# A routed-expert block: the slot's weight moves into the up rows, and the scattering matmuls are split into two FP32R parts

## The reference, cut to what matters

```python
g_onehot = one_hot(argmax(g_logits)); p_group = sum(softmax(g_logits) * g_onehot)
top_v, top_i = top_k(softmax(e_sel), 2); top_v = top_v / sum(top_v)
comb = g_onehot * w_local * p_group          # 0 but for the token's two experts
for g in range(N_GROUPS):
    a = silu(h @ w_gate[g]) * (h @ w_up[g])  # per expert, D_EXPERT = 256 columns
    a = a * comb[:, :, g, :, None]
    out = out + a @ w_down[g]
x = x + gate2 * out
```

## Time and profile before

| | |
|---|---|
| median of 3 runs | 501.27 us (500.9 to 501.34) |
| profiled execution, first to last instruction | 499.3 us |
| what lies around the span, against the median | 1.97 us |
| TensorE busy | 481.4 us, 96% |
| the windows, first to last gate/up start | 294.99 to about 486.8 us |
| one window where nothing waits | 5.31 us |
| bytes moved | 162.02 MB, 324 GB/s over the span |

### The profile page before, as it was taken

How to read it: one execution, slowest core, us unless ns; L and a number is a source line. 1 busy time by engine, 2 the same in 40 slices (tenths; PEclk the granted TensorE clock), 3 DMA queues, 4 the chain that set the end, 5 groups by cost and what they waited for, 6 DMA issues and landing times.

```text
span 499.3 us, 14059 instructions
## 1 busy us (share of the span) xinstructions
PE 481.4 (96%) x5769; PEld 378.1 (76%) x5770; DVE 241.3 (48%) x647; ACT 136.6 (27%) x243; POOL 152.8 (31%) x195
## 2 busy tenths in 40 slices
PE   8899999999999999999999999999999999888895
PEld 6678888888888888888888877767767766556563
DVE  1433765656565656456651455344344344332343
ACT  4013122323222232313232362232232232221231
POOL 0000010101010101010100018777777777665673
PEclk9999999999999999999999999999999999998998
DMA  8999318295969590907073999899999999999992
GB/s 324 423 424 425 164 53 379 58 433 202 427 258 425 219 407 25 408 8 296 42 291 130 362 411 430 358 394 422 434 437 427 421 441 427 421 423 428 424 403 95
DMA packets 13711, 162.02 MB, mean 324 GB/s; under 512 B 1648, under 2 KB 1904, under 8 KB 3568
## 3 DMA queue, kind: packets, MB, share of 16 engines
q1 hardware_dynamic: 13392, 161.04, 78.1%
q10 hardware_dynamic: 288, 0.52, 0.3%
HBM read 160.51 MB, written 1.05 MB: 324 GB/s over the span
## 4 chain that ended last, share of the span: by engine, by line
PE 83%; DMA 14%; DVE 2%; ACT 0%; issue 0%; ACTq 0%; DVEq 0%
PE ps L536 79%; DMA wex<-in_ex 14%; PE ps L839 1%; PE ps L879 1%; PE ps L840 1%; DVE work L958 0%; ACT xT L528 0%; PE ps L755 0%; PE ps L753 0%; PE ps L754 0%; DVE act L973 0%; DVE act L961 0%; PE ps L739 0%; ACT work L431 0%; DVE work L1223 0%
## 5 line engine op out<-in xcount | busy, mean ns | idle before, releaser
L536 PE MATMUL ps<-act,wmix 128*128 128x256 f32 x864 | 195.0, 381 | 1.7 <-DVE act L973 1.7
L536 PEld LDWEIGHTS ps<-act,wmix 128*128 128x128 f32 x864 | 161.1, 190 | 25.9 <-issue 4.6
L412 POOL TENSOR_SCALAR work<-trig,work 128x256 f32<-128x256 f32 x70 | 64.9, 937 | 57.3 <-issue 48.1
L398 POOL TENSOR_TENSOR work<-work,trig 64x256 f32<-64x256 f32 x8 | 5.8, 719 | 237.0 <-ACT work L466 141.6
L536 PE MATMUL ps<-work 32*128 32x256 f32 (+6 forms) x864 | 72.8, 374 | 0.6 <-DVE work L1223 0.6
L536 PE MATMUL ps<-wex,work 128*32 128x128 f32 (+1 forms) x1824 | 65.6, 295 | 3.7 <-DMA wex<-in_ex 3.7
L536 PEld LDWEIGHTS ps<-wex,work 128*32 128x32 f32 x1824 | 49.8, 110 | 16.8 <-issue 8.4
L536 PEld LDWEIGHTS ps<-work 32*128 32x128 f32 (+3 forms) x864 | 47.6, 168 | 13.3 <-issue 3.3
L524 ACT ACTIVATE work<-ps 128x64 f32<-128x64 f32 x35 | 7.8, 224 | 139.9 <-PE ps L879 139.9
L524 ACT ACT_TABLE_LOAD x35 | 44.9, 1283 | 1.8 <-issue 0.3
L416 POOL TENSOR_TENSOR work<-work,trig 128x512 f32<-128x512 f32 x35 | 44.5, 1271 | 0.0
(11 more groups left out here) (200 smaller groups left out, 432.2 us busy)
## 6 DMA issues: line engine op xcount, KB each, us to landing
wex<-in_ex SPq DMA_DIRECT2D x10, 3072.0 KB, 22.4
wex<-in_ex SPq DMA_DIRECT2D x10, 2048.0 KB, 24.1
wex<-in_ada SPq DMA_DIRECT2D x8, 2048.0 KB, 7.7
wmix<-in_ex SPq DMA_DIRECT2D x4, 3072.0 KB, 20.9
wmix<-in_mix_odd SPq DMA_DIRECT2D x4, 3008.0 KB, 15.5
wmix<-in_mix_even SPq DMA_DIRECT2D x3, 3200.0 KB, 16.1
wex<-in_ex SPq DMA_DIRECT2D x9, 1024.0 KB, 11.4
wex<-in_ada SPq DMA_DIRECT2D x8, 1024.0 KB, 16.7
```

What stands on the lines that cost most here:

```text
L398: nc.gpsimd.tensor_tensor(k_sq[0:ROPE, :], k_sq[0:ROPE, :], k_rope_sq[0:ROPE, :], ALU.add).then_inc(sq_joined, 1)
L412: nc.gpsimd.tensor_scalar(comb_both[:, rows], slot_row[:, rows], lane_now, None, ALU.is_equal).then_inc(comb_half, 1)
L536: return nc.tensor.matmul(out, lhsT, rhs, start=start, stop=stop, **kw)
```

## The change

- **Weight.** `comb` is no longer multiplied with `weight_row`; line 416 goes, and `comb` holds zeros and ones. Instead a column per window, `row_scale`, holds 1 in the gate partitions (0 to 63) and the slot's weight in the up partitions; DVE's copy at line 1208 becomes a product with column n of it.
- **Making row_scale.** Ahead of its loop POOL turns the four slot numbers of each partition's tokens into window and lane (five short operations, each waiting for the one ahead), then into two one-hot sets, of 32 lanes (four operations) and of 48 windows times the weight (four operations). TensorE multiplies them (8 matmuls of M=32, N=48) in the place of `spread(2, ...)`, and ACT copies 64 x 48.
- **Scattering.** DVE writes the down result times gate rows to `y_full`, copies it to `y_high` in FP32R and subtracts to `y_low` in FP32R; `comb` is FP32R too. `combine` multiplies low and high part with `comb`: 16 source matmuls in place of 8.
- Around it: three zeroing copies and a memset in place of one memset ahead of the router, `bound` at least 1 in TensorE's registers, `slot_no` 48 wide, and 8 KB for the DMA scratch.

```diff
-        ycomb = piece(2 * T)
-        y_sb, comb = ycomb[:, 0:T], ycomb[:, T:2 * T]
+        row_scale = sb("row_scale", [P, WINDOWS])
+        y_high, y_low, comb = (sb(n, [P, T], F32R) for n in ("y_high", "y_low", "comb"))
+        slot_row, y_full = trig[:, 0:2 * T], trig[:, 2 * T:3 * T]
@@ POOL, ahead of its loop
+            pool.wait_ge(slot_tok_ready, 1)
+            nc.gpsimd.tensor_scalar(win_no, slot_of, 1.0 / WIN, 0.5 / WIN - 0.5, ALU.mult, ALU.add).then_inc(pool_step, 1)
+            pool.wait_ge(pool_step, 1)
...
+            for a in range(4):
+                nc.gpsimd.tensor_scalar(lane_oh[:, a, :], co("slot_no")[:, 0:WIN], lane_of[:, a:a + 1], None, ALU.is_equal).then_inc(scale_in, 1)
+            pool.wait_ge(w_tok_ready, 1)
+            for a in range(4):
+                nc.gpsimd.tensor_scalar(win_oh[:, a, :], co("slot_no"), win_no[:, a:a + 1], w_of[:, a:a + 1], ALU.is_equal, ALU.mult).then_inc(scale_in, 1)
@@ POOL, in its loop
-                nc.gpsimd.tensor_tensor(comb_both, comb_both, weight_row, ALU.mult).then_inc(comb_pair, 1)
@@ ACT
-            nc.scalar.copy(weight_row, ps[:, 2, :]).then_inc(spread_copied, 1)
+            nc.scalar.copy(row_scale[P // 2:, :], ps[P // 2:, 2, 0:WINDOWS]).then_inc(spread_copied, 1)
@@ TensorE
-                return mm(ps[:, 4 + q, h * T:(h + 1) * T], y_sb[q * WIN:(q + 1) * WIN, h * P:(h + 1) * P], comb[q * WIN:(q + 1) * WIN, :],
-                          False, True, skip_group_check=True)
+                for y in (y_low, y_high):
+                    last = mm(ps[:, 4 + q, h * T:(h + 1) * T], y[q * WIN:(q + 1) * WIN, h * P:(h + 1) * P], comb[q * WIN:(q + 1) * WIN, :],
+                              False, True, skip_group_check=True)
+                return last
-            pe.wait_ge(w_tok_ready, 1)
-            spread(2, s_work[:, 8:10, :])
+            pe.wait_ge(scale_in, 8)
@@ DVE, in its loop
-                v.tensor_copy(gu_sb, ps[:, 0, 0:P]).then_inc(gu_copied, 1)
+                v.tensor_scalar(gu_sb, ps[:, 0, 0:P], row_scale[:, bass.ds(n, 1)], None, ALU.mult).then_inc(gu_copied, 1)
-                v.tensor_tensor(y_sb, ps[:, 2, 0:T], gate_rows, ALU.mult).then_inc(y_copied, 1)
+                v.tensor_tensor(y_full, ps[:, 2, 0:T], gate_rows, ALU.mult).then_inc(y_step, 1)
+                v.tensor_copy(y_high[:], y_full).then_inc(y_step, 1)
+                v.tensor_tensor(y_low[:], y_full, y_high[:].bitcast(F32), ALU.subtract).then_inc(y_copied, 1)
```

More of the change, by code:

```diff
@@ L8 @@
 U32 = mybir.dt.uint32
+F32R = mybir.dt.float32r
 ACT = mybir.ActivationFunctionType
@@ L35 @@
                 ("b_router", 36), ("w_router", KT * 36), ("gate_rows", T))
-CONST_WIDTHS = (("ident", P), ("before", P), ("swap", P), ("slot_no", WIN), ("lane_no", 1), ("mask", T),
+CONST_WIDTHS = (("ident", P), ("before", P), ("swap", P), ("slot_no", EXPERTS + 2 * T // WIN), ("lane_no", 1), ("mask", T),
                 ("group_no", GROUPS), ("less_magic", EXPERTS), ("fold", 37), ("inv_freq", 1))
@@ L170, in block_kernel @@
         logits_t, sq_sums = hT[:, 4, :], hT[:, 5, :]
+        lane_oh = comb_both[:, 0:4 * WIN].rearrange("p (a n) -> p a n", a=4)
+        win_oh = comb_both[:, 4 * WIN:4 * WIN + 4 * WINDOWS].rearrange("p (a n) -> p a n", a=4)
+        win_no, lane_of = comb_both[:, 2 * T - 8:2 * T - 4], comb_both[:, 2 * T - 4:2 * T]
         rs_tok, r_tok = s_work[:, 10, :], s_work[:, 11, :]
@@ L405, in _ @@
             with pool.Fori(0, windows_before(pool, EXPERTS)) as n:
-                pool.wait_ge(comb_pair, n * 2 + 1)
+                pool.wait_ge(comb_pair, n + 1)
                 pool.wait_ge(comb_ready, n + 1)
@@ L415, in _ @@
                 nc.gpsimd.tensor_scalar(lane_now, lane_now, float(WIN), None, ALU.add).then_inc(comb_pair, 1)
-                nc.gpsimd.tensor_tensor(comb_both, comb_both, weight_row, ALU.mult).then_inc(comb_pair, 1)
-                pool.wait_ge(comb_pair, n * 2 + 3)
                 pool.wait_ge(combined, n + 1)
-                nc.gpsimd.tensor_tensor(comb, comb_both[:, 0:T], comb_both[:, T:2 * T], ALU.add).then_inc(comb_ready, 1)
+                nc.gpsimd.tensor_tensor(comb[:], comb_both[:, 0:T], comb_both[:, T:2 * T], ALU.add).then_inc(comb_ready, 1)
         @block.scalar
@@ L861, in next_bound @@
                 pe.reg_mov(bound_at, bound)
-                pe.reg_mov(bound, bound_next)
+                pe.reg_alu(bound, bound_next, 1, ALU.max)
             def window(place, use, n, following, at_tail=False):
@@ L895, in _ @@
             pe.reg_mov(bound_at, 0)
-            pe.reg_load(bound, table[0:1, 1:2])
+            pe.reg_load(bound_next, table[0:1, 1:2])
+            pe.reg_alu(bound, bound_next, 1, ALU.max)
             turn_rows(0)
-            pe.wait_ge(w_tok_ready, 1)
-            spread(2, s_work[:, 8:10, :])
+            pe.wait_ge(scale_in, 8)
+            for a in range(4):
+                for q in (2, 3):
+                    last = mm(ps[q * WIN:(q + 1) * WIN, 2, 0:WINDOWS], lane_oh[:, a, :], win_oh[:, a, :], a == 0, a == 3)
+            last.then_inc(spread_ready, 1)
             ROUNDS = EXPERTS // EX_SLOTS
@@ L1111, in _ @@
             merge(HEADS - 1)
-            v.memset(ycomb, 0.0).then_inc(y_copied, 1)
+            v.memset(row_scale[0:P // 2, :], 1.0)
+            link(v.memset(zeros[:], 0.0))
+            for y in (y_high, y_low, comb):
+                last = v.tensor_copy(y[:], zeros[:].broadcast_to([P, T]))
+            last.then_inc(y_copied, 1)
             v.memset(wins[:, 0:1], 0.0)
@@ L1249, in constants @@
     put("lane_no", (r % WIN).astype(np.float32)[:, None])
-    put("slot_no", np.broadcast_to(np.arange(WIN, dtype=np.float32), (P, WIN)))
+    put("slot_no", np.broadcast_to(np.arange(WINDOWS, dtype=np.float32), (P, WINDOWS)))
     mask = np.zeros((P, T), np.float32)
```

27 lines of the change are left out of this document (20 added, 7 removed).

## The result

| | before | after |
|---|---|---|
| median | 501.3 us (500.9 to 501.98, 4 runs) | 510.53 us (509.94 to 512.72, 4 runs) |
| ratio | 1 | 1.0187, 95% interval 1.0162 to 1.0212 |
| span of the profiled execution | 499.3 us | 508.1 us |
| first gate/up | 294.99 | 303.28 |
| first refill of weights issued | 297.01 | 306.61 |

The account below looks back on a forecast made before the run. DMA is full and the end hangs on the last weights' landing. Start +1.55 and five combines at -0.41 move the issue by -0.50, the last gate/up by -1.13; with +0.05 at the end 500.2 us, range 498.4 to 503.8.

Parts of the forecast that it names:

- The start of the windows: Ahead of the first window, TensorE waits for POOL instead of running spread(2): first gate/up 1.55 us later, bounds 0.8 and 3.
- POOL's chain: POOL's operations making row_scale ahead of the loop: 2.1 plus 2.64 us from slots ready, so TensorE starts at 296.0.
- The clock: Rival: TensorE's clock drops after a wait, ahead of the last gate/up or at 294 us; costs 1.7, 501.9 us; chance 0.22.
- What bounds the kernel: In the windows DMA is full; early TensorE savings close a DMA hole at 322 to 326 us and pull landings in.
- The scattering matmuls: Each window's combine in one-pass FP32R takes 0.66 us instead of 1.07, 0.41 saved.
- no gain per combine: Rival: FP32R takes two passes, or low and high part on one row tile block the next; 503.7 us; chance 0.14.
- DVE and POOL in the window: In each window, DVE's added operations fit under existing cover and POOL's dropped product was not waited for: nothing.
- The last part: Behind the last gate/up: two combines at -0.41 each and y's two further DVE operations at +0.87, sum +0.05 us.
- Waits for weights: Sign: TensorE waits for weights about ten times, over 20 us in all, instead of 7.
- the hole closes entirely: Rival: start late by 0.8, combines shorter by 0.6, DMA hole at 322 us gone; 498.3 us; chance 0.12.

Follow-up runs that it names:

- the shortened kernel: The changed kernel with five warming matmuls of 512 columns instead of ten of 256, 20 TensorE instructions fewer ahead of the loop: 503.2 us, ratio 1.003.
- the one without padding: The changed kernel without the head_slot padding that puts the head of TensorE's outer loop at the start of a block of 256 instructions: 503.39 us.
- the kernel before with the wait: The kernel before with POOL's 13 new operations ahead of its loop, TensorE's wait for them and one register step more: 503.44 us.
- the weight alone: The shortened kernel with combine in float32 and one y as before, row_scale and the product in the copy kept: 504.69 us, ratio of four runs 1.0056.
- one of eight combine matmuls: The kernel before with seven of the eight combine matmuls left out in each window, the last combine whole: 498.07 us.
- the split alone: The kernel before with y in low and high part and 16 FP32R combine matmuls; weight_row, spread(2) and POOL's product kept: 500.06 us, ratio 0.9964.
- the version that beats both: The shortened kernel with row_scale made by eight POOL and two DVE operations, the last combine taking high parts first: 500.57 us, ratio 0.9974.
- changed, shortened, 20 put back: The shortened kernel with 20 TensorE instructions put back at the start as five matmuls of one column: 510.76 us.

## Why the prediction was wrong, point by point

**The start of the windows** is the step that failed. It gave +1.55 us, bounds 0.8 and 3; measured are +8.29 for the first gate/up and +9.6 for the first refill. Three things were wrong in it.
- *The branch, 6.0 us.* The term priced the eight small matmuls by their duration (0.5 us, measured 0.53) and not by the room that they take. The order showed 16 records more ahead of a loop with `head_slot` in it, and neither the step nor a rival asked what the padding does when code grows. The branch's 0.32 us could have been read from the trace of before. No bound from rows would have held 6 us, but a rival "the loop's head moves by a block" belonged in the list.
- *POOL's chain, +0.7 us.* TensorE was to start at 296.0 and started at 296.68, of which 0.31 are the prologue. The operations of 4 columns took 0.20 to 0.33, as expected from 0.22, and the gaps between them 0.1 instead of 0.20. The plain form took 0.36 for 32 columns instead of 0.31, the two-operation form 0.53 for 48 columns instead of 0.35, inside the bound ("at double").
- *The clock, 1.3 us.* The rival had it "in the new 2 us wait at 294 us" at 1.34 for a gate/up. In the changed kernel it came with 6 us of idle time, 1.31. After 2.2 us of idle time it came in the profiled executions of the shortened kernel and of the one without padding, and didn't in that of the kernel before with the wait, nor in the weight alone; so its chance is open, its price is right.

**What bounds the kernel** was right: DMA full, last landing 37.7 us behind its issue, the end hanging on it by a lag of TensorE that vanished (0.12 us). The kernel with most of each combine left out shows it best. The other half of the step, that all landings follow the issue behind the sixth gate/up, can be read from SP's timeline in each kernel; the last issue lands 37.7 or 37.8 us later in those where it was read. Starts in us, then differences from the kernel before:

| | first refill | issue behind the sixth gate/up | last gate/up issue |
|---|---|---|---|
| before | 297.01 | 323.89 | 448.29 |
| one of eight combine matmuls | -0.16 | -2.40 | -1.95 |
| the split alone | +0.32 | -0.79 | -0.57 |
| the version that beats both | +0.20 | -0.82 | -0.66 |
| changed, without the padding | +3.09 | +1.75 | +1.78 |
| changed, shortened | +3.97 | +2.62 | +4.37 |
| changed, shortened, 20 put back | +11.07 | +10.08 | +10.24 |
| changed | +9.60 | +7.92 | +9.42 |

In five of the seven the last issue moves with the middle column to within 0.5 us, and not with the first refill. In the profiled executions of the changed and of the shortened kernel it comes 1.5 and 1.75 later than that. These are one execution each, and near relatives of both don't show it; its cause stays open.

**The scattering matmuls**: 0.66 forecast, 0.69 measured, so 0.38 saved instead of 0.41; one pass. The four groups of four begin 0.23, 0.11 and 0.12 us apart. The window takes 4.93 us where nothing waits (combines begin at 307.59 and 312.52), forecast 4.9. The Trainium skill ("FP8 and Floating Point Precision", TensorE Precision Notes) gives four passes to true FP32 and knows a read at reduced precision beside it. Taken as one pass, that is the forecast's 0.66, and the trace agrees.

**The rival "no gain per combine"** falls: low and high part next to each other on one row tile don't hold up the next tile. The Trainium skill's rule of strict program order from start to end ("TensorE: Matmul & The Clock Gate", Part 3) would have made it 1.07. The 0.69 speaks against it for tiles in different rows, and so do the rows above, in which all four low parts begin ahead of the first high part.

**DVE and POOL in the window** at nothing: right in the changed kernel, where TensorE waits for neither in the windows. `y_low` took 0.58 in a window and 0.43 at the end, inside the bounds. With POOL's product kept, in the split alone, it was not free: 0.60 us once.

**The last part** at +0.05: the stretch from the last gate/up to the end is 12.53 us against 12.5. The final wait is 1.40 instead of 0.62, and the two combines give it back.

**Waits for weights**, about ten and over 20 us forecast: nine, 14.7 us. The late start is not the reason: the split alone began on time and waited 14.5 us in nine. The combines saved 35 x 0.38 = 13.3 us and the waits grew by 7.4; where the rest went stays open.

**The rival "the hole closes entirely"** has a slip in its price: two combines at -0.6 and +0.87 for `y` give back 0.33 at the end, not 0.6, so it is 498.4 us.

The sum with the measured terms: +8.29 for the start, +1.31 for the clock in the first gate/up and -5 x 0.38 for the combines put the issue behind the sixth gate/up at +7.70; it came at +7.92, and 0.22 is the gap at 315.29. The last landing is at +9.42, the 1.50 between them being the open part; then lag -0.65 and end +0.03: +8.8, as the spans say. But for the 1.50 the form of the prediction's sum holds; missing from its terms were 6.0 us for the branch, 1.3 for the clock and 0.7 for POOL's chain.

## What to carry to other kernels

Look in TensorE's instruction stream, not only in its busy time: where a loop's head is aligned, a few instructions ahead of it can cost 6 us, and taking a few away, or the alignment, brings them back. Long idle time with "issue" as its cause ahead of a loop is the sign, and the branch's own duration on the sequencer the proof. And when transfers are the bound, price an edit by what it does to the issue that ends the last hole in their stream, and ask whether a late start opens a new hole ahead of it; a saving on the engine that waits counts only up to the hole that it can close.

## What the runs showed of the hardware

- A branch to code that is not loaded: 6.0 us with the weight stream at full rate (5.99, 5.89, 6.01 in three kernels), 3.79 with DMA idle, 0.32 where the code is there. The code's packet is only 16 KB, but it started 3.55 us behind the branch under the full stream and 0.96 us behind it with DMA idle.
- The way back of the same loop, over seven experts, took 0.22 us each time, and no packet of TensorE's code queue stands between 354 and 478 us in the trace of the kernel after: the body was kept.
- An FP32R matmul with 32 rows and 256 columns is one pass: 16 of them on four row tiles in 0.69 us, against 1.07 for eight in float32. The four tiles overlap, and the trace has them begin out of program order. A single float32 one among other work still took 0.63 to its successor.
- On POOL a comparison with a product behind it took 0.52 to 0.54 us for 48 columns, the plain one 0.36 to 0.38 for 32 in the kernel after, both with 128 partitions.
- A DVE operation with two inputs over POOL's product of two inputs took 1.35 us (0.28 where POOL stood still), 0.96 in the kernel before.
